# Expert networks of a two-layer decoder trunk: gathered expert rows replaced by a dense pass over the expert tables

## The chip, the cores and the metric

The kernel runs as one program on one core of a Trainium2 chip. The core has five engines that run side by side and meet through semaphores: TensorE (PE) multiplies 128-row matrices, with loaded weights on one side and up to 512 moving columns on the other, and writes to PSUM; VectorE (DVE) and ScalarE (ACT) do elementwise work; GpSimd (POOL) and SyncE (SP) issue DMA transfers here. The metric is the device time of one execution in microseconds (us); lower is better. The change touches no other core.

## The reference, cut to what matters

Two layers; each is a mixer, a cross-attention and an expert network, all in float32, for 256 tokens of width 1024. The change concerns the expert network (PEER), which for each token picks 16 experts in each of 8 heads out of 16384:

```python
q = (xi @ wq).reshape(Tb, PEER_HEADS, 2, PEER_DQ // 2)
s = jnp.einsum('thcd,hcnd->thcn', q, subkeys).astype(jnp.float32)
s1, i1 = lax.top_k(s[:, :, 0], K)          # K = 16 of 128 keys, each half
s2, i2 = lax.top_k(s[:, :, 1], K)
cand = (s1[..., :, None] + s2[..., None, :]).reshape(Tb, PEER_HEADS, K * K)
cidx = (i1[..., :, None] * PEER_NKEYS + i2[..., None, :]).reshape(Tb, PEER_HEADS, K * K)
top_s, pos = lax.top_k(cand, K)
eidx = jnp.take_along_axis(cidx, pos, axis=-1)
g = jax.nn.softmax(top_s, axis=-1)
ue = u[eidx]                               # u, v: (16384, 1024) per layer
ve = v[eidx]
act = jax.nn.gelu(jnp.einsum('td,thkd->thk', xi, ue).astype(jnp.float32), approximate=False)
return jnp.einsum('thk,thkd->td', (g * act).astype(ve.dtype), ve)
```

Each token so needs 128 rows of `u` and 128 of `v`. An expert's number is 128 * i1 + i2.

## The kernel before

Activations are kept with features on partitions (`xT`, `hT`: 8 blocks of 128 features by 256 tokens). Weights come in blocks of 2 MB through a `ring` of four, loaded by SP in the fixed order of `weight_blocks`; a block is loaded once the last PSUM job that reads the one four before it is full. All of PE's work is a list of named PSUM jobs (`psum_jobs`); job n uses bank n % 8 and waits until that bank's last user has set it free. The order of that list is PE's order.

The expert network of a layer (`peer(l)` on PE, ACT and DVE, and the GpSimd block) has two parts. First four groups g of queries: two jobs `pq` (16 float32 matmuls each, 256 columns), in the first two groups two `xr` jobs that transpose `hT` to token rows (`xrow`), and two `ps` jobs (4 matmuls each of 128 columns: the key scores of 128 tokens). DVE picks the best keys (`best_keys`), forms and sorts the candidate pairs (`candidates`, `best_pairs`, `ranks`) and turns them into expert numbers (`chosen`), two heads at a time for the first 128 tokens, and between units for the other 128.

Then 256 units per layer. A unit is one expert slot of 128 tokens, one token per partition: GpSimd gathers for each partition the 8 KB row that holds `u` and `v` of its expert (`indirect_dma_start`, 1 MB, eight slots in `arena`); DVE multiplies the `u` half by the token's row and sums it (`unit`, L1416); ACT takes Gelu, multiplies by the gate and scales an identity matrix by the result (`diag`, four buffers, L882); PE multiplies this diagonal with the `v` half, two matmuls of 512 columns, which add up over 128 units in two banks (`acc`, L516). ACT copies the sum out, PE transposes it (`back`) and DVE adds it to `xT` (L1423). The helper `mm` on PE is line L516 and the helper `fn` on ACT line L882 for every job, so that rows are told apart by their tiles. In a row of PE the names are all tiles read, in no fixed order, and one float32 `mm` stands as two records of MATMUL: the 512 units make 1024 calls of `mm` and about 2048 records.

Of the kernel before, what the change touches and what calls it, by code (L numbers as in the profile page):

```python
# [15 lines left out]
D = 1024  # L16
# [18 lines left out]
EXPERTS = PE_KEYS * PE_KEYS  # L35
# [23 lines left out]
for _name, _n in (("ident", P), ("ones", P), ("head_ones", P), ("rot", P), ("tri", P),  # L59
                  ("past", 3 * P), ("causal", 3 * P), ("iota", PE_K), ("inv_freq", 1),  # L60
                  ("levels", 8 * P)):
    CONSTS[_name] = (sum(n for _, n in CONSTS.values()), _n)
# [3 lines left out]
SLOTS = 8  # L66
UNITS = PAIRS * TT
DIAGS = 4

# [4 lines left out]
LATE_EXP = 64  # L74
BACK_LAG = 4


def constants():
# [26 lines left out]
    put("iota", np.broadcast_to(np.arange(PE_K), (P, PE_K)))  # L105
# [42 lines left out]
X_ROWS = ((0, 1), (2, 3), (), ())  # L148
# [4 lines left out]
def psum_jobs():  # L153
# [59 lines left out]
def trunk(nc, d, out_d):  # L213
# [8 lines left out]
    with ExitStack() as ctx:  # L222
# [12 lines left out]
        ring = sb("ring", [P, RING, BLOCK])  # L235
        arena = sb("arena", [P, 16384])
        vecs = sb("vecs", [P, NVEC])
        cst = sb("cst", [P, NCONST])
        w_gg = sb("w_gg", [P, KC, GLA_RANK])
        gate_up = sb("gate_up", [GLA_RANK, 2 * P])  # L240
        w_rg = sb("w_rg", [P, 2, 4, P])
# [5 lines left out]
        red = sb("red", [P, T])  # L247
        rstd = sb("rstd", [P, T])
        small = sb("small", [P, 256])
        idxT = sb("idxT", [P, T], U32)  # L250
        gateT = sb("gateT", [P, T])
        xrow = sb("xrow", [P, TT, D])
        gelus = sb("gelus", [P, SLOTS])
        gains = sb("gains", [P, SLOTS])
# [47 lines left out]

        mhV = carve(0, KC, M)
# [24 lines left out]
        late = mixT[:].rearrange("p c t -> p (c t)")  # L328
# [4 lines left out]
        s16 = sqb[:, 1024:1280].rearrange("p (c k) -> p c k", k=PE_K)  # L333
# [6 lines left out]
        i16 = rstd[:].bitcast(U32).rearrange("p (c k) -> p c k", k=PE_K)  # L340
        eidx = red[:, 0:PAIRS]

        slot = [arena[:, j * 2 * D:(j + 1) * 2 * D] for j in range(SLOTS)]

        yrow = kv[:, 0:D]
        dots = red[:, PAIRS:2 * PAIRS]

        diag = const('levels').rearrange('p (n m) -> p n m', m=P)[:, 0:DIAGS, :]

# [8 lines left out]
        in_mem = sem("in_mem")  # L358
        act_chain, dve_chain = sem("act_chain"), sem("dve_chain")
# [38 lines left out]
        routed = sem("routed")  # L398
        idx_ready = sem("idx_ready")

        gathered = [sem(f"gathered{j}") for j in range(SLOTS)]
        dotted = sem("dotted")
        gelu_done = sem("gelu_done")
        gain_done = sem("gain_done")
        weighed = sem("weighed")
        expert_mm = sem("expert_mm")
# [23 lines left out]
        def back_jobs(l):  # L430
            return [f"back{l}.{t}.{b}" for t in range(TT) for b in range(2)]

# [15 lines left out]
        def slot_of(u):  # L448
            return (u + 1) % SLOTS

        def landed(eng, l, u):

            eng.wait_ge(gathered[slot_of(u)], 16 * (l * UNITS // SLOTS + u // SLOTS + 1))

        def taken(eng, l, u):

            eng.wait_ge(expert_mm, l * UNITS + u + 1)
# [3 lines left out]
        def _(sp):  # L461
# [1319 lines left out]
```

## Time and profile before

| | us |
|---|---|
| median of 3 runs | 1932.83 |
| lowest and highest | 1928.16 and 1933.31 |
| span of the profiled execution | 1928.8 |
| PE busy | 1591.4 (83%) |
| DVE busy | 1011.3 (52%) |
| ACT busy | 646.9 (34%) |
| POOL busy | 514.9 (27%) |
| mean DMA rate | 316 GB/s |

The record has no time for the profiled execution other than its span, which lies among the times of the runs. Busy time counts records of compute instructions; matmuls overlap each other by their latency, so that busy PE means only that there was something in it. An average over the span mixes the projections, where PE works without DMA, with the two expert stages.

### The profile page before, as it was taken

Reading aid. Unit: us, or ns where it says so; the run is one execution under the profiler, and the core shown is the slowest. Engines: PE = TensorE matmul, PEld = TensorE weight load, DVE = VectorE, ACT = ScalarE, POOL = GpSimd, SP = SyncE. Lnnn points to the kernel's source line nnn. Section 1 sums busy time; section 2 is a strip of 40 time slices with the busy share of each in tenths; the row PEclk is TensorE's granted clock in tenths of the full one; section 3 lists DMA queues with packets and bytes.
Section 4 is the critical chain, followed back from the end, with each engine's and each line's share of the span. In section 5 each row is a group of like instructions: output and inputs, shape, how many; then the busy total and the mean of one; then the engine's idle time right before and its main releaser. Section 6 shows DMA issues by size and latency. Waiting matters only on the chain.

```text
span 1928.8 us, 15560 instructions
## 1 busy us (share of the span) xinstructions
PE 1591.4 (83%) x4638; PEld 806.3 (42%) x4638; DVE 1011.3 (52%) x2487; ACT 646.9 (34%) x1897; POOL 514.9 (27%) x516
## 2 busy tenths in 40 slices
PE   7999989767877877787779989997788777877876
PEld 4777778222322222222237666763232222222222
DVE  3432238688544554445441632489874445444454
ACT  1243221423433333333332433123343333333333
POOL 0000001434433433333300000015444343333331
PEclk9999999999999999999989999999999999999999
DMA  8321224999999999999933222359999999999996
GB/s 304 131 88 44 101 108 184 390 416 421 422 421 422 421 422 422 421 421 422 421 154 131 88 104 93 118 221 422 421 421 421 422 421 421 422 421 422 421 421 287
DMA packets 107540, 610.20 MB, mean 316 GB/s; under 512 B 10032, under 2 KB 10176, under 8 KB 41280
## 3 DMA queue, kind: packets, MB, share of 16 engines
q0 software_dynamic: 73728, 536.90, 67.1%
q1 hardware_dynamic: 33728, 72.30, 10.3%
q8 instruction: 37, 0.61, 0.1%
q14 instruction: 47, 0.39, 0.1%
HBM read 608.12 MB, written 1.05 MB: 316 GB/s over the span
## 4 chain that ended last, share of the span: by engine, by line
DMA 45%; PE 38%; DVE 9%; ACT 5%; issue 2%; POOL 0%; SPq 0%; DVEq 0%; PEldq 0%; ACTq 0%
DMA arena<-in_experts,idxT 45%; PE psum L516 37%; DVE arena L1416 5%; ACT cst L882 1%; ACT gains L882 1%; ACT arena L882 1%; ACT gelus L882 1%; ACT L882 1%; DVE red L1385 1%; DVE kv L1377 0%; POOL arena L1710 0%; DMA vecs<-in_vecs 0%; ACT sqb L882 0%; DVE kv L1383 0%; DVE red L1200 0%
## 5 line engine op out<-in xcount | busy, mean ns | idle before, releaser
L516 PE MATMUL psum<-arena,cst 128*128 128x512 f32 (+2 forms) x2112 | 1029.4, 616 | 283.6 <-ACT cst L882 279.1
L1416 DVE CUSTOM_DVE_ANT_0 arena<-arena,xrow 128x1024 f32<-128x1024 f32 x512 | 624.4, 1224 | 537.7 <-DMA arena<-in_experts,idxT 537.0
L1710 POOL DMA_INDIRECT arena<-in_experts,idxT x512 | 514.7, 1005 | 1387.8 <-PE psum L516 790.0
L516 PEld LDWEIGHTS psum<-arena,cst 128*128 128x128 f32 x2112 | 367.1, 191 | 942.5 <-ACT cst L882 645.7
L882 ACT ACTIVATE gelus<-red 128x1 f32<-128x1 f32 x512 | 103.6, 202 | 770.2 <-DVE red L1416 769.9
L516 PE MATMUL psum<-hT,ring 128*128 128x256 f32 x1280 | 293.3, 390 | 6.1 <-DVE hT L1215 6.1
L516 PEld LDWEIGHTS psum<-hT,ring 128*128 128x128 f32 x1280 | 248.9, 196 | 47.5 <-issue 9.8
L882 ACT ACTIVATE cst<-cst,gains 128x128 f32<-128x128 f32 x512 | 206.2, 403 | 23.2 <-PE psum L516 6.7
L882 ACT ACTIVATE gains<-gelus,gateT 128x1 f32<-128x1 f32 x512 | 150.8, 294 | 17.0 <-ACT gelus L882 0.2
L882 ACT ACTIVATE arena<-psum 128x512 f32<-128x512 f32 (+3 forms) x89 | 47.8, 545 | 304.3 <-PE psum L516 304.0
L516 PE MATMUL psum<-mixT,ring 128*128 128x256 f32 x256 | 57.4, 387 | 2.5 <-DVE mixT L1689 2.5
L516 PE MATMUL psum<-arena 64*128 64x128 f32 (+4 forms) x320 | 52.0, 317 | 4.9 <-DVE arena L1521 2.4
L516 PEld LDWEIGHTS psum<-mixT,ring 128*128 128x128 f32 x256 | 49.7, 195 | 10.8 <-DVE mixT L1689 3.3
L1223 DVE TENSOR_TENSOR xT<-xT,psum 128x512 f32<-128x512 f32 x16 | 11.0, 688 | 72.8 <-PE psum L516 72.8
L516 PE MATMUL psum<-ring,arena 128*128 128x128 f32 (+1 forms) x192 | 44.6, 384 | 2.9 <-issue 2.9
L516 PEld LDWEIGHTS psum<-arena 64*128 64x128 f32 (+2 forms) x320 | 35.7, 177 | 20.0 <-issue 10.5
L1416 DVE DVE_READ_ACCUMULATOR2_ANT red<- 128x1 f32 x512 | 42.5, 83 | 0.0
L516 PE MATMUL psum<-ring,hT 128*128 128x512 f32 x96 | 42.3, 595 | 0.0
L882 ACT ACTIVATE sqb<-xT 128x512 f32<-128x512 f32 x24 | 14.4, 625 | 81.2 <-DVE xT L1223 77.3
L516 PEld LDWEIGHTS psum<-ring,arena 128*128 128x128 f32 x192 | 27.1, 191 | 18.3 <-issue 17.8
L1533 DVE COPY_PREDICATED arena<-cst,psum 128x512 f32<-128x512 int32 x16 | 11.7, 730 | 40.7 <-PE psum L516 40.4
L516 PE MATMUL psum<-arena,ring 128*128 128x256 f32 x128 | 28.1, 380 | 1.6 <-ACT arena L882 1.6
(161 smaller groups left out, 672.1 us busy)
## 6 DMA issues: line engine op xcount, KB each, us to landing
ring<-in_peer_wq SPq DMA_DIRECT2D x8, 2048.0 KB, 8.1
ring<-in_ev_w_in SPq DMA_DIRECT2D x6, 2048.0 KB, 11.8
ring<-in_od_w_in SPq DMA_DIRECT2D x5, 2048.0 KB, 33.0
ring<-in_xa_wkv SPq DMA_DIRECT2D x4, 2048.0 KB, 7.9
arena<-in_experts,idxT POOLq DMA_INDIRECT x512, 15.3
ring<-in_ev_w_out SPq DMA_DIRECT2D x2, 2048.0 KB, 7.8
ring<-in_xa_wq SPq DMA_DIRECT2D x2, 2048.0 KB, 9.2
ring<-in_xa_wo SPq DMA_DIRECT2D x2, 2048.0 KB, 7.7
```

The costliest lines, as they stand in the source:

```text
L516: return nc.tensor.matmul(out, lhsT, rhs, start=start, stop=stop)
L882: return nc.scalar.activation(out, in_, f, **k)
L1223: V.tensor_tensor(x2, x2, pairs(o), ALU.add).then_inc(bank_free(name), 1)
L1385: link(V.tensor_reduce(eidx[:, cols], h_.rearrange("p (n c) j -> p n (c j)", c=2), X, ALU.add))
L1416: V.tensor_tensor_reduce(out=ut, in0=ut, in1=xrow[:, u // PAIRS, :], scale=1.0, scalar=0.0, op0=ALU.mult, op1=ALU.add, accum_out=dots[:, k ...
L1533: ins = V.copy_predicated(attn[:, par].rearrange("p a t q -> p (a t) q"), msk, o.rearrange("p (n q) -> p n q", q=P))
L1710: nc.gpsimd.indirect_dma_start(slot[slot_of(u)], None, d["experts"], bass.IndirectOffsetOnAxis(ap=idxT[:, u:u + 1], axis=0))\
```

## The change

The 8 KB gathers, the unit's dot products, the diagonals and the GpSimd block go. In their place all 16384 experts are computed for all 256 tokens:

- **Tables.** `keys_u` and `values_v` (64 MB each per layer) come as 128 chunks of 512 KB each, row i1 of experts per chunk, through four slots (two in `mixT`, two in `stream_tail`), issued by SP.
- **Score jobs** `pu` (64 per layer): two chunks each; for a chunk 8 matmuls, the chunk's 128x128 blocks as weights and `hT` as 256 moving columns. ACT takes Gelu of the bank into `rows_`, a field of 128 rows i1 by 256 tokens that covers `ring` and `arena`.
- **Routing.** The choice of experts keeps its instructions but gives i1, i2 and the softmax weight per slot (`picked`); three transposes per half (`tr`, after score jobs 15 and 21) turn it. From score job 22 on, `pg` jobs (64 per layer, 4 tokens each, 8 in 5 score jobs) multiply two one-hot matrices that DVE makes (`onehots`, 8 instructions of 128x128 for a job), which gives the gates of a token as a 128x128 matrix. Where the field's row is already scored DVE multiplies (`gate_rows`); for the later rows ACT copies the gates into the field, and the later scores are multiplied in (`gate_acts`).
- **Values.** After the last score job 4 matmuls with the identity put `xT` into four banks, and 128 chunks of `values_v` follow, 8 matmuls of 256 columns each, that add to the four banks (`acc`).
- **Around it.** Ring blocks are loaded in 4 parts; layer 1's first four blocks are loaded in parts between the value chunks, each part when the field's rows in its place have been read. The residual is now a copy (`whole`). The output leaves in four parts. The level masks live in `arena`, and `w_rg` is loaded after layer 0.

```diff
+STREAM = 4
+PARTS = 4
+SCORE_JOBS = PE_KEYS // 2
+GATE_TOKENS = 4
+GATE_JOBS = T // GATE_TOKENS
+EXP_AT = (9, 16)
+FLIP_AT = (15, 21)
+GATE_FROM = 22
+def gates_upto(s):
+    return min(GATE_JOBS, max(0, (8 * (s - GATE_FROM + 1) + 4) // 5))
+def gates_after(s):
+    return range(gates_upto(s - 1), gates_upto(s))
+def gated(s):
+    return GATE_TOKENS * gates_upto(s - 1)
...
     def peer(l):
         for g in range(4):
-            jobs.extend([f"pq{l}.{2 * g}", f"pq{l}.{2 * g + 1}"] + [f"xr{l}.{n}" for n in X_ROWS[g]])
-            jobs.extend([f"ps{l}.{g}", f"ps{l}.{4 + g}"])
-        jobs.extend(f"acc{l}.{t}.{b}" for t in range(TT) for b in range(2))
-        jobs.extend(f"back{l}.{t}.{b}" for t in range(TT) for b in range(2))
+            jobs.extend([f"pq{l}.{2 * g}", f"pq{l}.{2 * g + 1}", f"ps{l}.{g}", f"ps{l}.{4 + g}"])
+        for s in range(SCORE_JOBS):
+            jobs.append(f"pu{l}.{s}")
+            jobs.extend(f"tr{l}.{t}" for t in range(TT) if s == FLIP_AT[t])
+            jobs.extend(f"pg{l}.{g}" for g in gates_after(s))
+        jobs.extend(f"acc{l}.{i}" for i in range(4))
...
+            def stream(l, n):
+
+                m = n - STREAM
+                if m < 0:
+                    full(sp, "ev_out3" if l == 0 else "od_out3")
+                    if l:
+                        full(sp, f"acc{l - 1}.3")
+                elif m < PE_KEYS and m % 2:
+                    full(sp, f"pu{l}.{m // 2}")
+                elif m < PE_KEYS:
+                    sp.wait_ge(keys_read, SCORE_JOBS * l + m // 2 + 1)
                 else:
+                    sp.wait_ge(values_read, (PE_KEYS - 1) * l + m - PE_KEYS + 1)
+                table = d["keys_u"] if n < PE_KEYS else d["values_v"]
+                sp.dma_start(slots[slot_of(l, n)], table[PE_KEYS * l + n % PE_KEYS])\
+                    .then_inc(stream_in[slot_of(l, n)], 16)
...
+                for s in range(SCORE_JOBS):
+                    o, done = job(f"pu{l}.{s}")
+                    for j in range(2):
+                        u = streamed(pe, l, 2 * s + j).rearrange("p (k e) -> p k e", e=P)
+                        for k in range(KC):
+                            last = mm(o[:, j * T:(j + 1) * T], u[:, k, :], hT[:, k, :], k == 0, k == KC - 1)
+                        last.then_inc(done if j else keys_read, 1)
...
+                    for g in gates_after(s):
+                        pe.wait_ge(hot_ready, GATE_JOBS * l + g + 1)
+                        o, done = job(f"pg{l}.{g}")
+                        for j in range(GATE_TOKENS):
+                            last = mm(o[:, j * P:(j + 1) * P], onehot[:, g % 2, 0, j, :], onehot[:, g % 2, 1, j, :])
                         last.then_inc(done, 1)
-                for t in range(TT):
-                    (o0, done0), (o1, done1) = job(f"acc{l}.{t}.0"), job(f"acc{l}.{t}.1")
-                    for k in range(PAIRS):
-                        u = t * PAIRS + k
-                        pe.wait_ge(weighed, l * UNITS + u + 1)
-                        v = slot[slot_of(u)][:, D:2 * D]
-                        first = mm(o0, diag[:, u % DIAGS, :], v[:, 0:BANK], k == 0, k == PAIRS - 1)
-                        last = mm(o1, diag[:, u % DIAGS, :], v[:, BANK:D], k == 0, k == PAIRS - 1)
...
+                acc = [job(f"acc{l}.{i}") for i in range(4)]
+                for i in range(4):
+                    mm(acc[i][0], ident, xT[:, 2 * i:2 * i + 2, :].rearrange("p c t -> p (c t)"), True, False)
+                copied(pe, f"pg{l}.{GATE_JOBS - 1}", f"pu{l}.{GATED_FROM - 1}")
+                for i in range(PE_KEYS):
+                    if i // 2 >= GATED_FROM:
+                        pe.wait_ge(acts_gated, GATED_JOBS * l + i // 2 - GATED_FROM + 1)
+                    v = streamed(pe, l, PE_KEYS + i)
+                    for c in range(KC):
+                        o, done = acc[c // 2]
+                        last = mm(o[:, c % 2 * T:(c % 2 + 1) * T], v[:, c * P:(c + 1) * P], rows_[:, i, :],
+                                  False, i == PE_KEYS - 1 and c % 2 == 1)
...
+                def onehots(g):
+
+                    if g >= 2:
+                        n = JOB[f"pg{l}.{g - 2}"]
+                        dve.wait_ge(psum_full[n % BANKS], n // BANKS + 1)
+                    copied(dve, f"tr{l}.{GATE_TOKENS * g // P}")
+                    for j in range(GATE_TOKENS):
+                        t = GATE_TOKENS * g + j
+                        step(V.tensor_scalar(onehot[:, g % 2, 0, j, :], const("iota"), pickT[:, 1, t:t + 1], None, ALU.is_equal))
+                        ins = V.tensor_scalar(onehot[:, g % 2, 1, j, :], const("iota"), pickT[:, 0, t:t + 1],
+                                              pickT[:, 2, t:t + 1], ALU.is_equal, ALU.mult)
...
+                def gate_rows(s, g):
+
+                    o = full(dve, f"pg{l}.{g}").rearrange("p (t i) -> p i t", i=PE_KEYS)
+                    dve.wait_ge(gate_copied, GATE_JOBS * l + g + 1)
+                    copied(dve, f"pu{l}.{s}")
+                    x_ = rows_[:, 0:2 * s + 2, GATE_TOKENS * g:GATE_TOKENS * (g + 1)]
+                    V.tensor_tensor(x_, x_, o[:, 0:2 * s + 2, :], ALU.mult).then_inc(bank_free(f"pg{l}.{g}"), 1)
...
+                for s in range(GATE_FROM, SCORE_JOBS):
+                    if gated(s):
+                        gate_acts(s)
+                    for g in gates_after(s):
+                        gate_rows(s, g)
+                        if g + 2 < GATE_JOBS:
+                            onehots(g + 2)
```

On PE, at the end of layer 0's queries and in its expert stage, the kernel before has these rows (`psum<-` names the tiles read; `hT,ring` is a `pq` job, `ring,arena` a `ps` job, `arena,cst` the units, `cst,kv` a `back` job; one row counts calls of `mm`):

```order
L516 MATMUL psum<-hT,ring 128x256 x32
L516 MATMUL psum<-ring,arena 128x128 x8
L516 MATMUL psum<-hT,ring 128x256 x32
L516 MATMUL psum<-ring,arena 128x128 x8
L516 MATMUL psum<-arena,cst 128x512 x268
L663 MATMUL psum<-cst,kv 128x128 x8
L516 MATMUL psum<-arena,cst 128x512 x244
L663 MATMUL psum<-cst,kv 128x128 x8
```

The changed kernel has there, at the end of the score jobs and the start of the values (`hT,mixT` and `hT,stream_tail` are `pu` jobs, `sqb` the one-hot products of `pg`, `xT,cst` the identity matmuls, `field` the rows of activations):

```order
L577 MATMUL psum<-hT,mixT 128x256 x16
L577 MATMUL psum<-sqb 128x128 x8
L577 MATMUL psum<-hT,stream_tail 128x256 x16
L577 MATMUL psum<-sqb 128x128 x4
L577 MATMUL psum<-hT,mixT 128x256 x16
L577 MATMUL psum<-hT,stream_tail 128x256 x16
L577 MATMUL psum<-xT,cst 128x512 x4
L577 MATMUL psum<-field,mixT 128x256 x16
L577 MATMUL psum<-field,stream_tail 128x256 x16
```

Where 512 calls of 512 columns stood per layer, there stand 64 groups of 16 calls of 256 columns for the scores, 64 groups of 4 calls of 128 columns for the gates, 4 of 512 columns, and 128 groups of 8 calls of 256 columns for the values.

On DVE, in the same stretch of score jobs, the changed kernel has rows of this kind (`field<-field,kv` is `gate_acts`, `field<-field,psum` is `gate_rows`, `sqb<-cst,pick` are the one-hots, eight of them before the next `gate_rows`):

```order
L1480 TENSOR_TENSOR field<-field,kv 128x2x104
L1472 TENSOR_TENSOR field<-field,psum 128x78x4
L1459 TENSOR_SCALAR sqb<-cst,pick 128x128
L1460 TENSOR_SCALAR sqb<-cst,pick 128x128
L1459 TENSOR_SCALAR sqb<-cst,pick 128x128
```

They take the place of the dot products (L1416) of the units, 256 a layer.

## Rows read from the trace of the kernel before

**Rows 1.** The page, parts 1 and 2: busy time; DMA rate in 40 slices

```profile
PE 1591.4 (83%) x4638; PEld 806.3 (42%) x4638; DVE 1011.3 (52%) x2487; ACT 646.9 (34%) x1897; POOL 514.9 (27%) x516
GB/s 304 131 88 44 101 108 184 390 416 421 422 421 422 421 422 422 421 421 422 421 154 131 88 104 93 118 221 422 421 421 421 422 421 421 422 421 422 421 421 287
```

**Rows 2.** The page, part 4: the chain that ended last, by engine

```profile
DMA 45%; PE 38%; DVE 9%; ACT 5%; issue 2%; POOL 0%; SPq 0%; DVEq 0%; PEldq 0%; ACTq 0%
```

**Rows 3.** Groups of instructions by line and shape, whole span

```profile
L516 PE MATMUL psum<-arena,cst 128*128 128x512 f32 x2064 | 1018.2, 622 | 283.6 <-ACT cst L882 279.1 <-ACT arena L882 4.4
L1416 DVE CUSTOM_DVE_ANT_0 arena<-arena,xrow 128x1024 f32<-128x1024 f32 x512 | 624.4, 1224 | 537.7 <-DMA arena<-in_experts,idxT 537.0
L516 PE MATMUL psum<-hT,ring 128*128 128x256 f32 x1280 | 293.3, 390 | 6.1 <-DVE hT L1215 6.1
```

**Rows 4.** The timeline of expert units, steady state of layer 0

```profile
599.33 1.98 PE L516 MATMUL psum<-arena,cst 128*128 128x512 f32 x4 [0.51 <-ACT cst L882]
599.53 1.23 DVE L1416 CUSTOM_DVE_ANT_0 arena<-arena,xrow 128x1024 f32<-128x1024 f32 x1 [1.25 <-DMA arena<-in_experts,idxT]
601.81 1.98 PE L516 MATMUL psum<-arena,cst 128*128 128x512 f32 x4 [0.50 <-ACT cst L882]
```

**Rows 5.** Busy time in the two expert stages (columns named in the row)

```profile
core 0: us, PE busy (x) PEld busy (x) DVE busy (x) ACT busy (x) POOL busy (x), PEclk, DMA share, GB/s
338.30:1001.70 663.40, 511.28 (x1043) 180.62 (x1042) 375.72 (x829) 244.47 (x791) 248.53 (x249) 0.98 0.98 407
1283.90:1928.80 644.90, 504.14 (x1041) 179.74 (x1040) 371.97 (x820) 239.34 (x781) 252.93 (x249) 0.99 0.98 407
```

**Rows 6.** The timeline of PE, end of layer 0's queries

```profile
302.24 1.04 PE L644 MATMUL psum<-cst,hT 128*128 128x128 f32 x8
303.14 2.02 PE L516 MATMUL psum<-ring,arena 128*128 128x128 f32 x16
305.00 13.98 PE L516 MATMUL psum<-hT,ring 128*128 128x256 f32 x64
319.71 2.02 PE L516 MATMUL psum<-ring,arena 128*128 128x128 f32 x16 [0.73 <-issue]
```

**Rows 7.** The timeline of PE in layer 1's mixer

```profile
1037.95 3.60 PE L516 MATMUL psum<-sqb,cst 128*128 128x512 f32 x8
1041.39 7.07 PE L516 MATMUL psum<-hT,ring 128*128 128x256 f32 x32
```

**Rows 8.** Busy time and granted clock, two stretches (columns as in rows 5)

```profile
270.00:275.00 5.00, 5.00 (x14) 4.00 (x13) 1.69 (x5) 0.00 (x0) 0.00 (x0) 0.54 0.32 116
1045.00:1085.00 40.00, 40.00 (x151) 27.21 (x150) 18.49 (x39) 8.73 (x15) 0.00 (x0) 1.00 0.40 142
```

**Rows 9.** Groups of instructions by line and shape, VectorE, whole span

```profile
L1223 DVE TENSOR_TENSOR xT<-xT,psum 128x512 f32<-128x512 f32 x16 | 11.0, 688 | 72.8 <-PE psum L516 72.8
L1650 DVE TENSOR_SCALAR sqb<-sqb,small 128x128 f32<-128x128 f32 x8 | 2.3, 286 | 0.3
```

**Rows 10.** The timeline of VectorE: first and last instruction routing two heads

```profile
287.73 0.89 DVE L1293 MAX8 sqb<-psum 128x8 f32<-128x128 f32 x4 [16.04 <-PE psum L516]
...
301.59 0.18 DVE L1386 CAST idxT<-red 128x32 uint32<-128x32 f32 x1
```

**Rows 11.** The page, part 6: DMA issues, size and time to landing

```profile
arena<-in_experts,idxT POOLq DMA_INDIRECT x512, 15.3
ring<-in_subkeys SPq DMA_DIRECT2D x2, 1024.0 KB, 4.9
```

**Rows 12.** The timeline between a projection's end and the next, layer 0

```profile
264.31 0.69 DVE L1223 TENSOR_TENSOR xT<-xT,psum 128x512 f32<-128x512 f32 x1 [1.97 <-PE psum L516]
269.07 1.19 PE L516 MATMUL psum<-hT,ring 128*128 128x256 f32 x2 [1.53 <-DVE hT L1215]
```

**Rows 13.** The timeline of the kernel's last expert work and output

```profile
1919.63 1.98 PE L516 MATMUL psum<-arena,cst 128*128 128x512 f32 x4 [0.47 <-ACT cst L882]
1924.48 0.36 SPq L492 DMA_DIRECT2D out<-xT  x1
```

More of the change, by code:

```diff
@@ L34 @@
 PE_H, PE_K, PE_KEYS, PE_DQ = 8, 16, 128, 128
-EXPERTS = PE_KEYS * PE_KEYS
 PAIRS = PE_H * PE_K
@@ L339, in trunk @@
         row_a, row_at, line = sqb[:, 1792:1920], sqb[:, 1920:2048], sqb[:, 1536:1664]
[L340 to L348, printed above, removed]
+        onehot = sqb[:].rearrange("p (b c j n) -> p b c j n", b=2, c=2, j=GATE_TOKENS)
+        acts = kv[:].rearrange("p (b i t) -> p b i t", i=2, t=T)
+        slots = [mixT[:, 0:4, :].rearrange("p c t -> p (c t)"), mixT[:, 4:8, :].rearrange("p c t -> p (c t)")]
+        slots += [stream_tail[:, j, :] for j in range(STREAM - 2)]
         psum = ctx.enter_context(nc.psum_tensor("psum", [P, BANKS, BANK], F))
@@ L397, in trunk @@
         top_exp = sem("top_exp")
[L398 to L406, printed above, removed]
+        picked_ready = sem("picked_ready")
+        stream_in = [sem(f"stream_in{j}") for j in range(STREAM)]
+        keys_read, values_read = sem("keys_read"), sem("values_read")
+        hot_ready = sem("hot_ready")
+        gate_copied = sem("gate_copied")
+        acts_gated = sem("acts_gated")
         stored = sem("stored")
@@ L486, in _ @@
             load(3)
-            sp.dma_start(w_rg[:], d["rg_gates"]).then_inc(in_mem, 16)
             sp.dma_start(sinT[:].bitcast(I32), d["positions"].to_broadcast([P, T])).then_inc(in_mem, 16)
-            for b in range(RING, len(BLOCKS)):
+            first = AT["od_mq"]
+            for b in range(RING, AT["pq02"]):
                 load(b)
-            copied(sp, "back1.1.0", "back1.1.1")
-            sp.dma_start(out_d, xT[:]).then_inc(stored, 16)
-            sp.wait_ge(stored, 16)
+            for n in range(STREAM):
+                stream(0, n)
+            for b in range(AT["pq02"], first):
+                load(b)
+            for n in range(STREAM, 2 * PE_KEYS):
+                stream(0, n)
+                i, ahead = divmod(n - PE_KEYS - 40, 4)
+                if ahead == 0 and 0 <= i < RING * PARTS:
+                    b = first + i // PARTS
+                    if i % PARTS == 0:
+                        sp.wait_ge(values_read, BLOCK // T * (b % RING + 1))
+                    part(b, i % PARTS)
+            full(sp, "acc0.3")
+            sp.dma_start(w_rg, d["rg_gates"]).then_inc(in_rg, 16)
+            for b in range(first + RING, AT["pq12"]):
+                load(b)
+            for n in range(STREAM):
+                stream(1, n)
+            for b in range(AT["pq12"], len(BLOCKS)):
+                load(b)
+            for n in range(STREAM, 2 * PE_KEYS):
+                stream(1, n)
+            for i in range(4):
+                copied(sp, f"acc1.{i}")
+                sp.dma_start(out_d[:, 2 * i:2 * i + 2, :], xT[:, 2 * i:2 * i + 2, :]).then_inc(stored, 16)
+            sp.wait_ge(stored, 64)
         @block.tensor
@@ L1010, in peer, with exponentials, activate @@
-                rows_out(1)
+                def exponentials(t):
+                    act.wait_ge(top_ready, TT * l + t + 1)
+                    fn(top, top, ACT.Exp).then_inc(top_exp, 1)
+                def activate(s):
+                    n = gated(s)
+                    o = full(act, f"pu{l}.{s}").rearrange("p (i t) -> p i t", t=T)
+                    if n < T:
+                        ins = fn(rows_[:, 2 * s:2 * s + 2, n:], o[:, :, n:], ACT.Gelu)
+                    if n:
+                        m = s - GATED_FROM
+                        if m >= 4:
+                            act.wait_ge(acts_gated, GATED_JOBS * l + m - 3)
+                        ins = fn(acts[:, m % 4, :, 0:n], o[:, :, 0:n], ACT.Gelu)
+                    ins.then_inc(bank_free(f"pu{l}.{s}"), 1)
@@ new lines, in peer @@
+                for s in range(SCORE_JOBS):
+                    activate(s)
+                    for t in range(TT):
+                        if s == EXP_AT[t]:
+                            exponentials(t)
+                        if s == FLIP_AT[t]:
+                            copy_out(f"tr{l}.{t}", pickT[:, :, t * P:(t + 1) * P])
+                    for g in gates_after(s):
+                        o = full(act, f"pg{l}.{g}").rearrange("p (t i) -> p i t", i=PE_KEYS)
+                        ts = slice(GATE_TOKENS * g, GATE_TOKENS * (g + 1))
+                        fn(rows_[:, 2 * s + 2:, ts], o[:, 2 * s + 2:, :], ACT.Copy).then_inc(gate_copied, 1)
@@ L1593, in _ @@
             peer(0)
+            residual(parts("acc0.", 4), "od", whole=True)
             norm("od", xT, vec("od_norm"), hT, h_ready)
```

331 lines of the change are left out of this document (121 added, 210 removed).

## The prediction

> **What bounds the kernel now.** I read the page first: PE is busy 83% of the span, DVE half of it, and the DMA rate stands at 421 GB/s in two long plateaus [rows 1]. The chain that ended last gives 45% of the span to one transfer, the gather of expert rows, and 38% to PE [rows 2]. The groups say what each engine waited for: the dot products for the gather (537.0 us), the diagonal matmuls for ACT (279.1 us), which itself stands behind the dot product [rows 3]. The timeline settles it: units start 2.48 us apart (599.33 to 601.81), and in that time PE has 1.98 us of records and DVE 1.23 us; DVE waits 1.25 us for the DMA each time [rows 4]. 1 MB in 2.48 us is 422 GB/s, the plateau. So the two expert stages, 663.4 us in layer 0 (end of the last key scores to the first matmul of the next projection) and 644.9 us in layer 1 (to the end), are bound by DMA [rows 5]; 256 x 2.48 = 635 us of each is gathers. The other 620.5 us of the span are projections and attention, which the change hardly touches.
>
> The bytes halve: 128 MB for a layer instead of 256 MB. At 422 GB/s that is 318 us. The question is whether PE can follow, so what matters is the price of one float32 matmul.
>
> **The price of a matmul.** Where nothing interrupts PE, the end of the queries, 64 records of 128x256 last 13.98 us in all [rows 6]; one record has 0.390 us from issue to end [rows 3], so starts are (13.98 - 0.39) / 63 = 215.7 ns apart. The 32 records in rows 7 give (7.07 - 0.39) / 31 = 215.5. The code issues 640 calls of `mm` with `hT` and a ring block at 256 columns, and the trace has 1280 records [rows 3]: one call is two records, 431.4 ns. The units count the same way, 1024 calls and some 2048 records. For 512 columns, 8 records take 3.44 us to the next row's start [rows 7], 0.86 us a call. For 128 columns, 16 records from 303.14 to 305.00 are 0.2325 us a call [rows 6]. The transposes are one record each, 8 in 0.90 us [rows 6].
>
> The Trainium skill, "FP8 and Floating Point Precision", TensorE Precision Notes, says that true FP32 takes four passes through the array, and "TensorE: Matmul & The Clock Gate", section "Wait — 56ns, not 53.3ns?", puts a warm matmul of N columns at N / 2.4 GHz plus about 2.5 ns. By four such passes a call of 256 columns would be an estimated 4 x 109.2 = 437 ns, which makes the sum below 22 us longer; by a single pass it would be 109 ns and the change would win widely. The measured 431.4 sides with four passes, and the sum goes by it.
>
> **What is added, per layer.** All new `mm` calls of the scores have the form of the queries (128x128 weights from SBUF, `hT` as 256 moving columns), and the values have the same shape with the field's row as moving side:
> - scores 64 x 16 and values 128 x 8 = 2048 calls x 0.4314 = 883.5 us
> - gates 64 x 4 = 256 calls x 0.2325 = 59.5 us
> - 6 transposes 0.7 us, 4 identity calls x 0.86 = 3.4 us
> - together 947.1 us of PE, without a gap.
>
> **What hides the rest.** Transfers: a chunk of 512 KB is used up in 8 x 0.4314 = 3.45 us, 152 GB/s. A slot is refilled while PE is on the other three, 10.35 us. The nearest direct load, 1 MB, lands in 4.9 us [rows 11], so this is hidden, also with the weight parts between them. DVE in the gate stretch: for five score jobs there are eight `pg` jobs. Per score job 12.8 one-hots of 128x128 at most 0.286 us each = 3.66 us, 1.6 `gate_rows` and one `gate_acts` of at most 0.69 us each = 1.79 us [rows 9]: 5.5 us, while PE takes 16 x 0.4314 + 6.4 x 0.2325 = 8.4 us. The order also fits: after a `pg` is full, its `gate_rows` and the one-hots of the job after the next follow in about 3 to 6 us, and a score job of 6.9 us lies between. Routing: two heads of 128 tokens take DVE 14.0 us [rows 10], eight such parts 112 us; they start with the first key scores, some 50 us before the score jobs, so that both halves could be ready 62 us into them. The exponentials hold them back (ACT does them after score jobs 9 and 16, at 69 and 117 us), but PE asks for the halves only after jobs 15 and 21, at 110 and 152 us. ACT has two Gelu halves and at most two copies in 8.4 us. I cost all of this at nothing. The four `xr` transposes per layer, 0.90 us for two of them, save little, since the key scores behind them have to wait 0.73 us for ACT where they are absent [rows 6]: 0.17 x 4 = 0.7 us in all.
>
> **The seams.** After layer 0's values comes the chain copy, squares, sums, norm, normalise. The same chain after a projection took from 264.31 to 269.07, 4.8 us [rows 12]. Layer 0: 947.1 + 4.8 = 951.9 instead of 663.4, +288.5 us. In layer 1 the last matmul is followed by one copy (0.69 us) and 256 KB of output. The 1 MB output was issued at 1924.48 and the span ended at 1928.8 [rows 13], 4.3 us; for less data I take 3.3, so a tail of 4 us. Layer 1: 951.1 instead of 644.9, +306.2 us.
>
> Sum: 1928.8 + 288.5 + 306.2 - 0.7 = 2522.8 us against the profiled span. The median of the runs shown is 4 us above that span; I take half of it: **2525 us**, 31% slower. The gathers were moving bytes that the dense form partly saves, but it trades 635 us of DMA for 947 us of PE.
>
> **The rivals.**
> - *The mean of the group instead of the uninterrupted pace.* All 1280 records occupy 293.3 us [rows 3], 0.458 a call, with the clock's dips and gated starts in it. Against it: the dips stand behind idle time (granted clock 0.54 at 270 to 275 us, after the wait of rows 12), and 40 us without a gap show 1.00 [rows 8]. The new stage has no idle stretch. If 256 stops for a chunk's semaphore per layer cost something, it would come out here: 4096 x 0.027 = +110, 2633 us. 60 ns a chunk would give +31, 2556. Chance 12% for something over 2585.
> - *The chunks come late.* If a chunk took the 15.3 us of the gathers [rows 11], a round of four would take 18.75 us instead of 13.8, 1.24 us more a chunk, 512 chunks: +634, 3160 us. It decides from 10.35 us on. The 15.3 belongs to up to eight transfers of 1 MB in flight at 421 GB/s; here at most four of half the size at 152. 2%.
> - *DVE or ACT bounds the gate stretch.* The field is written in runs of four elements, 1 KB apart, and PSUM is read across; no row has such a form. If `gate_rows` cost five times its row, DVE would need 9.9 us for PE's 8.4: +1.5 x 40 x 2 = +120, 2645 us. It decides from 2.5 us an instruction on, 3.6 times the row. 4%.
> - *The clock.* With PE granted its lower level, 1.2 GHz (0.50), over the whole stage every call doubles: some 4400 us. Nothing in the rows shows that without idle time ahead. 1%.
> - *Not slower.* If one `mm` of the new form were one record, not two, PE would need 2048 x 0.2157 + 63.6 = 505 us a layer, still above the 318 us of DMA, and the time would be 1928.8 - 1308.3 + 2 x 505 + 8.8 - 0.7 = 1639 us. It decides where a call costs less than (1308.3 + 0.7 - 8.8 - 127.2) / 4096 = 0.286 us. For it speaks only that the moving side of the values is new; against it every float32 group of the trace, the diagonals included, which have two records a call. 1%.
>
> **The numbers.** The sum as worked out holds with 80%: its own bounds are 2505 (tail and seam shorter, the 0.43 us a call to the third digit, the 0.2325 of the gates 10% high, the start a little shorter by the split loads) and 2585 (60 ns a chunk, a few dips after seams, 10 us of stalls while the gate stretch starts). The rest lies above, but for 1% below. Range 2500 to 2590. A measurement of this kernel tells 0.3% (6 us) from no change; by these cases faster has 1%, within it 1%, slower 98%.
>
> **What would show it.** In the profile after: the expert stages 950 us each; PE busy near 100% there with the clock at 1.00; 64 records in about 13.8 us also for `hT,mixT`; DMA at 150 GB/s in them; no wait of PE on the streams, on `hot_ready` or `picked_ready` worth more than a few us; DVE about 65% busy between the first `pg` and the last; the chain that ended last nearly all PE. Wrong would make it: records with another pace than 216 ns, waits of PE on a DMA of `mixT` or `stream_tail`, or on DVE's one-hots; or 1280-record counting that doesn't hold, so that the new stages have half the records.

## The result, and the profile after

The changed kernel took 2522.99 us (median of 4 runs, 2521.83 to 2524.73) against 1930.79 us for the kernel before beside it (4 runs, 1928.16 to 1933.31). The ratio is 1.3068, with an interval of 1.3048 to 1.3088: slower by 31%. The profiled span is 2522.9 us; 2525 was predicted, with a range of 2500 to 2590.

The page of the changed kernel, busy time, DMA rate in 40 slices and the chain that ended last, answers to [rows 1, 2]:

```profile
PE 2467.5 (98%) x11770; PEld 2119.1 (84%) x11770; DVE 685.1 (27%) x2503; ACT 297.4 (12%) x669; POOL 0.2 (0%) x4
GB/s 258 110 58 139 78 89 154 143 133 124 127 126 126 142 150 177 198 184 184 153 90 116 99 118 34 151 150 138 130 126 126 125 126 151 155 154 150 152 155 135
PE 97%; DVE 1%; ACT 1%; issue 1%; DMA 0%; SPq 0%; DVEq 0%
```

The plateau of 421 GB/s is gone. Nothing but PE is left in the chain, and DMA, which had 45% of it, has 0%. The groups by line and shape show the new work and how often each record stands (answers to [rows 3]; two more groups of 2048, with the other names, have the same means):

```profile
L577 PE MATMUL psum<-hT,mixT 128*128 128x256 f32 x2048 | 452.6, 379 | 0.0
L577 PE MATMUL psum<-field,stream_tail 128*128 128x256 f32 x2048 | 452.5, 379 | 0.0
L577 PE MATMUL psum<-sqb 128*128 128x128 f32 x1024 | 127.2, 275 | 0.0
L1460 DVE TENSOR_SCALAR sqb<-cst,pick 128x128 f32<-128x128 f32 x512 | 173.7, 339 | 0.0
L1459 DVE TENSOR_SCALAR sqb<-cst,pick 128x128 f32<-128x128 f32 x512 | 142.6, 278 | 0.1
```

4096 calls of 256 columns gave 8192 records: two for a call, as counted before. The last column, the idle time ahead of the group, is the strongest line of the page: in 8192 records on streamed chunks PE never waited. The price of a call stands in the timeline of PE in the changed kernel, in the gate stretch and in the values:

```profile
497.60 1.95 PE L577 MATMUL psum<-sqb 128*128 128x128 f32 x16
499.39 7.07 PE L577 MATMUL psum<-hT,stream_tail 128*128 128x256 f32 x32
506.30 1.95 PE L577 MATMUL psum<-sqb 128*128 128x128 f32 x16
508.08 7.07 PE L577 MATMUL psum<-hT,mixT 128*128 128x256 f32 x32
```

A score job of 16 calls takes 499.39 to 506.30, 6.91 us, 0.432 a call. Two gate jobs (8 calls) take 506.30 to 508.08, 1.78 us, 0.2225 a call. By the same reading a call of 512 columns takes 0.86 us (837.95 to 841.38 below, four calls). All three have 128x128 weights, so the price goes with the columns that move and not with the weights that are loaded. The windows of the changed kernel, over the scores, over the gate stretch, and over the values (columns as in rows 5):

```profile
338.00:830.00 492.00, 492.00 (x2533) 439.97 (x2532) 218.04 (x855) 66.10 (x173) 0.00 (x0) 1.00 0.42 134
516.00:800.00 284.00, 284.00 (x1530) 255.91 (x1529) 137.36 (x522) 39.84 (x123) 0.00 (x0) 1.00 0.40 127
840.00:1280.00 440.00, 440.00 (x2037) 386.69 (x2036) 0.00 (x0) 0.66 (x4) 0.00 (x0) 1.00 0.52 168
```

PE is busy for the whole of every window at a granted clock of 1.00, the 2.4 GHz level. DVE is busy 137.36 of 284 us in the gate stretch, 48%. The DMA issues of the page, size and time to landing, answer to [rows 11]:

```profile
mixT<-in_keys_u SPq DMA_DIRECT2D x128, 512.0 KB, 3.4
stream_tail<-in_values_v SPq DMA_DIRECT2D x128, 512.0 KB, 3.5
```

The borders of the stages stand in the timeline: first scores, identity calls, values, the seam, the first scores of layer 1, and the end (kernel after, answers to [rows 6, 12, 13]):

```profile
338.09 7.07 PE L577 MATMUL psum<-hT,mixT 128*128 128x256 f32 x32
...
837.95 3.60 PE L577 MATMUL psum<-xT,cst 128*128 128x512 f32 x8
841.38 7.07 PE L577 MATMUL psum<-field,mixT 128*128 128x256 f32 x32
...
1276.50 7.07 PE L577 MATMUL psum<-field,stream_tail 128*128 128x256 f32 x32
1286.73 0.70 PE L577 MATMUL psum<-sums,cst 128*128 128x256 f32 x2 [3.16 <-DVE sums L1259]
...
1573.98 7.07 PE L577 MATMUL psum<-hT,mixT 128*128 128x256 f32 x32
...
2519.51 0.69 DVE L1740 COPY xT<-psum 128x512 f32<-128x512 f32 x1 [0.17 <-PE psum L577]
```

The stage of layer 0 goes from 338.09 to the next projection's first matmul at 1288.96, 950.9 us; from there to layer 1's scores it is 285.0 us; layer 1's stage is 1573.98 to 2522.9, 948.9 us.

### The profile page after: what moved, and what is told of

Read it like the earlier page. It is cut to its first block, busy times and chain, and to the rows that moved or that the text cites. A ratio compares the mean times of both kernels' runs of the same rounds, so it can differ in the third digit from the quotient of the medians.

```text
span 2522.9 us, 28446 instructions
## 1 busy us (share of the span) xinstructions
PE 2467.5 (98%) x11770; PEld 2119.1 (84%) x11770; DVE 685.1 (27%) x2503; ACT 297.4 (12%) x669; POOL 0.2 (0%) x4
## 4 chain that ended last, share of the span: by engine, by line
PE 97%; DVE 1%; ACT 1%; issue 1%; DMA 0%; SPq 0%; DVEq 0%
PE psum L577 96%; ACT field L949 1%; DMA vecs<-in_vecs 0%; ACT sqb L949 0%; DVE sums L1259 0%; DVE sums L1258 0%; ACT sums L949 0%; DVE small L1314 0%; DVE field L1680 0%; ACT L949 0%; DVE field L1728 0%; PE psum L665 0%; DVE hT L1274 0%; DVE small L1683 0%; DVE small L1682 0%
## 5 line engine op out<-in xcount | busy, mean ns | idle before, releaser
L577 PE MATMUL psum<-hT,mixT 128*128 128x256 f32 x2048 | 452.6, 379 | 0.0
L577 PE MATMUL psum<-hT,stream_tail 128*128 128x256 f32 x2048 | 452.6, 379 | 0.0
L577 PE MATMUL psum<-field,stream_tail 128*128 128x256 f32 x2048 | 452.5, 379 | 0.0
L577 PE MATMUL psum<-field,mixT 128*128 128x256 f32 x2048 | 452.5, 379 | 0.0
L577 PEld LDWEIGHTS psum<-field,mixT 128*128 128x128 f32 x2048 | 389.1, 190 | 53.8 <-issue 1.0
L577 PEld LDWEIGHTS psum<-field,stream_tail 128*128 128x128 f32 x2048 | 389.1, 190 | 52.9
L577 PEld LDWEIGHTS psum<-hT,stream_tail 128*128 128x128 f32 x2048 | 386.1, 190 | 50.8
L577 PEld LDWEIGHTS psum<-hT,mixT 128*128 128x128 f32 x2048 | 385.6, 190 | 50.5
L577 PE MATMUL psum<-hT,field 128*128 128x256 f32 x1280 | 295.8, 393 | 6.1 <-DVE hT L1274 6.1
L1460 DVE TENSOR_SCALAR sqb<-cst,pick 128x128 f32<-128x128 f32 x512 | 173.7, 339 | 0.0
L1459 DVE TENSOR_SCALAR sqb<-cst,pick 128x128 f32<-128x128 f32 x512 | 142.6, 278 | 0.1
L1480 DVE TENSOR_TENSOR field<-field,kv 128x512 f32<-128x512 f32 (+39 forms) x82 | 36.2, 441 | 344.8 <-ACT kv L949 344.8
```

The costliest lines, as they stand in the source:

```text
L577: return nc.tensor.matmul(out, lhsT, rhs, start=start, stop=stop)
L1459: step(V.tensor_scalar(onehot[:, g % 2, 0, j, :], const("iota"), pickT[:, 1, t:t + 1], None, ALU.is_equal))
L1460: ins = V.tensor_scalar(onehot[:, g % 2, 1, j, :], const("iota"), pickT[:, 0, t:t + 1], pickT[:, 2, t:t + 1], ALU.is_equal, ALU.mult)
L1480: V.tensor_tensor(x_, x_, acts[:, m % 4, :, 0:n], ALU.mult).then_inc(acts_gated, 1)
```

## The experiments

The theory: a float32 call of 256 columns costs PE 0.431 us of its own, and 4096 of them are the whole loss; the transfers, DVE and ACT lie beside it with room. The rivals: the loss, or part of it, is in how the chunks arrive or in what DVE must make. A second question is why the old kernel stood where it did. Each run was timed beside the kernel before on the same chip. The edits are shown by their main lines; "..." stands for lines left out.

### The values in bf16

GpSimd loads pairs of chunks with a cast to bf16 (1 MB read, 512 KB written), the field is bf16, and the values' 1024 calls a layer run on bf16 operands; scores and gates stay float32 up to the field. The result is rounded accordingly. The narrower field leaves the ring free, so layer 1's first four weight blocks are loaded whole, from the eighth pair of layer 0's values on.

```diff
-        rows_ = field[:].rearrange("p (i t) -> p i t", t=T)
+        rows_ = arena.bitcast(BF).rearrange("p (i t) -> p i t", t=T)
...
+                    nc.gpsimd.dma_start(pair_slots[at % STREAM], table[i:i + 2].rearrange("i p d -> p i d"))\
+                        .then_inc(pair_in[at % STREAM], 16)
...
```

> Only the value matmuls are given bfloat16 operands: the field of activations is written as bfloat16, and GpSimd issues the value chunks in pairs (1 MB read, cast on the way). The scores stay float32. Theory (a float32 call is two records and 431 ns because of its type, and PE alone sets the expert stage): a bfloat16 call is one record of well under 216 ns, so that the transfer takes over as the bound of the value part: 64 pairs x 2.48 us = 159 us for a layer in place of 442, 2523 - 2 x 283 = 1957 us; value part with PE waiting for DMA. Rival A (the pace belongs to loading 128x128 weights, about 190 ns a load): 64 x 16 x 0.19 = 195 us, 2029 us, PE without a gap. Rival B (a cast transfer issued by GpSimd runs at half the rate): 317 us for a layer, 2273 us. Rival C (pace independent of the type): 2523 us.

Measured: 1982.84 us (1981.88 to 1983.8, 2 runs), ratio 1.0271 (1.025 to 1.0291). That is 540 us less than the changed kernel, from one half of its calls. The timeline of PE in this kernel, layer 1, from the last score job into the values:

```profile
1807.90 7.07 PE L601 MATMUL psum<-hT,stream_tail 128*128 128x256 f32 x32
1814.80 3.60 PE L601 MATMUL psum<-xT,cst 128*128 128x512 f32 x8
1818.24 3.66 PE L601 MATMUL psum<-field,mixT 128*128 128x256 bf16 x32
1821.73 3.66 PE L601 MATMUL psum<-field,stream_tail 128*128 128x256 bf16 x32
1826.04 1.92 PE L601 MATMUL psum<-field,mixT 128*128 128x256 bf16 x16 [0.66 <-DMA mixT<-in_values_v]
```

And in layer 0, while the weight blocks come in beside the values:

```profile
885.70 1.92 PE L601 MATMUL psum<-field,stream_tail 128*128 128x256 bf16 x16 [1.97 <-DMA stream_tail<-in_values_v]
889.59 1.92 PE L601 MATMUL psum<-field,mixT 128*128 128x256 bf16 x16 [1.97 <-DMA mixT<-in_values_v]
```

In the first list the first and the fourth row have the same shape and the same number of records, 7.07 us against 3.66: records now start 109 ns apart ((1821.73 - 1818.24) / 32), and a call has one record instead of two. After four pairs PE is ahead of the transfers and waits, so that the rivals fall: under rival A PE would have no gap, and B and C are 290 us and more above the measured time. The total is 26 us above what was expected, and most of it can be read in the trace: layer 0's values took from 841.27 to 1023.71, 182.4 us, layer 1's from 1818.24 to about 1977.4, 159 us. The 64 MB of a table at 422 GB/s are 159 us. Beside layer 0's values come the next layer's first four weight blocks, 8 MB or 20 us at that rate. They are issued from 858.53 on, and from there to about 925 the pairs start some 3.9 us apart instead of 2.48 (second list). In the changed kernel they are read under a PE that is busy anyway. I had left them out of a stage that this edit made DMA-bound. A speedup of PE turned hidden bytes into time.

### Scores in bf16 too

The edit before stays, and the scores run on bf16 keys, cast on the way, and a bf16 copy of `hT`.

```diff
+        at_b = [ring[:, AT[f"sub{l}"] % RING, 2048:3072].bitcast(BF).rearrange("p (k t) -> p k t", t=T) for l in range(LAYERS)]
...
-                            last = mm(o[:, j * T:(j + 1) * T], u[:, k, :], hT[:, k, :], k == 0, k == KC - 1)
+                            last = mm(o[:, j * T:(j + 1) * T], u[:, k, :], at_b[l][:, k, :], k == 0, k == KC - 1)
```

> Scores and values both have bfloat16 operands (a bfloat16 copy of the normalised activations for the scores; keys and values cast on the way, GpSimd issues them in pairs). Routing, gates and all else stay float32. Theory: PE no longer bounds the score part; DVE does, with 112 us of routing of which 50 lie before the score jobs, 512 one-hots at 0.23 us and 64 products, some 60 + 118 + 40 = 220 us, and values at the transfer's pace 159 us: 385 us for a layer in place of 947, total about 1400 us, faster than the kernel before by a quarter or more. Rival (one of the float32 parts that are left keeps PE as the bound, or the cast transfers run at half rate): 640 us for a layer, 1900 us or more.

Measured: 1412.4 us (1410.67 to 1415.61, 4 runs), ratio 0.7313 (0.7301 to 0.7325). The same dense plan, with the same number of calls and the same table bytes read, is 27% below the old kernel once the calls on the tables cost 109 ns. The old kernel keeps float32 operands in this comparison; no run has gathers with bf16 operands. What bounds it now differs by stretch. The timeline of PE in this kernel, in the values, and what PE waited for (us in total, times, longest):

```profile
648.60 1.91 PE L606 MATMUL psum<-field,mixT 128*128 128x256 bf16 x16 [0.56 <-DMA mixT<-in_values_v]
651.08 1.91 PE L606 MATMUL psum<-field,mixT 128*128 128x256 bf16 x16 [0.57 <-DMA mixT<-in_values_v]
```

```profile
PE psum L606 <- DMA mixT<-in_values_v: 47.6, 60, 2.1
PE psum L606 <- DMA stream_tail<-in_values_v: 45.0, 60, 2.0
PE psum L606 <- DVE sqb L1492: 36.1, 46, 1.3
```

Pairs are 2.48 us apart, the same 1 MB in 2.48 us that the gathers had [rows 4]. In the values PE waits for DMA; in the gate stretch it waits for DVE's one-hots, which the float32 calls had covered.

### A quarter of the gate products

```diff
                     for g in gates_after(s):
...
-                        for j in range(GATE_TOKENS):
+                        for j in range(1):
```

This leaves out PE's gate products of three tokens in four.

> Each gate job on PE multiplies the one-hots of one of its four tokens; the gates of the other three are left out (what stands in the bank is used). All waits and all work of DVE and ACT stay. Theory (PE bounds the gate stretch): 3/4 of the gates' 256 calls go, 2 x 192 x 0.2225 = 85 us less, 2438 us. Rival (DVE or the handshake of PE, ACT and DVE sets the pace of the stretch and PE's one-hot products are covered): 2523 us, or at most 20 us less.

Measured: 2436.53 us (2436.42 to 2436.64, 2 runs), ratio 1.2621 (1.2595 to 1.2646). It is 86.5 us less, for 384 calls of 128 columns less: 0.225 us a call. The whole of what is left out comes back, so PE sets the time in this stretch also, and it is the product's own price.

### DVE's one-hots three times

```diff
-                    for j in range(GATE_TOKENS):
+                    for n, j in enumerate([0, 1, 2, 3] * 3):
+                        if n in (GATE_TOKENS, 2 * GATE_TOKENS):
+                            settle()
...
```

Each one-hot is made three times over, with the same values. `settle` is a wait of DVE for its own last instruction, twice in each job.

> DVE makes every one-hot three times, with the same result. Theory (DVE is covered by PE, about 4.1 us of 8.35 us a score job in the gate stretch): DVE then needs 3 x 2.9 + 1.2 = 9.9 us a score job and a little more for its waits, and becomes the bound by 1.5 to 2.5 us, 40 score jobs in each layer: +120 to +200 us, 2640 to 2720 us, with PE waiting for DVE only in this stretch. Rival (DVE was at its limit already): + 2 x 40 x 5.8 = 464 us or more, 2990 us.

Measured: 2662.4 us (2661.83 to 2662.96, 2 runs), ratio 1.3791 (1.3763 to 1.3818). PE's wait for the one-hots in this kernel, and a window of its gate stretch (columns as in rows 5):

```profile
PE psum L577 <- DVE sqb L1462: 91.2, 43, 3.9
```

```profile
800.00:860.00 60.00, 53.72 (x252) 47.30 (x253) 59.37 (x236) 5.33 (x19) 0.00 (x0) 0.89 0.28 88
```

DVE is now busy for 59.37 us of the 60. Only what goes beyond PE's time is paid: in the changed kernel DVE has some 4.1 us in a score job's 8.4 (48%), of which 6.4 pairs of one-hots are 2.9 (a pair starts every 0.45 us, below); with three times the pairs DVE has 9.8 us. 1.4 us over in each of some 80 score jobs gives about 112 us, and 139 were measured. Most of the rest is the edit's own: around each `settle` the next one-hot starts 0.13 us later than within a round (699.97 to 700.35 is 0.38 us, where 524.88 to 525.13 in the changed kernel is 0.25), twice in each of 128 jobs, 33 us. PE's waits are only 91.2 us; its score and gate records take some 50 us longer in all, at a granted clock of 0.89 to 0.97 in the windows of this stretch, where the changed kernel has 1.00. By the same numbers the cover over DVE ends at about 2.5 times the present one-hots ((8.4 - 1.2) / 2.9), an estimate that no run tests; the changed kernel did not use it up.

### Two slots instead of four

```diff
-STREAM = 4
+STREAM = 2
...
-        stream_tail = sb("stream_tail", [P, STREAM - 2, D])
```

> The float32 dense kernel with two stream slots in place of four; the rest as it is. A slot is then refilled while PE is on one other chunk, 3.45 us (with four: 10.35 us). Theory (a chunk lands in about 3.5 us, so four slots cover it three times over): a turn of two chunks takes max(6.9, 3.45 + 3.5 + some 0.3 for the semaphores and the issue) = 7.2 us, +0.1 to 0.3 us a chunk, 512 chunks: 2555 to 2680 us, with short waits of PE for the streams. Rival (a chunk in flight alone is as slow as the gathers were, 15.3 us): a turn of 18.8 us, some 3000 us more.

Measured: 2638.2 us (2636.89 to 2639.51, 2 runs), ratio 1.3662 (1.3634 to 1.3689): 115 us more, 0.225 us for each of 512 chunks. The waits of PE in this kernel, and two rows of its timeline in layer 0's values:

```profile
PE psum L576 <- DMA mixT<-in_values_v: 36.2, 78, 1.4
PE psum L576 <- DMA mixT<-in_keys_u: 17.5, 39, 1.3
```

```profile
860.58 7.07 PE L576 MATMUL psum<-field,mixT 128*128 128x256 f32 x32
867.81 7.17 PE L576 MATMUL psum<-field,mixT 128*128 128x256 f32 x32 [0.16 <-DMA mixT<-in_values_v]
```

The waits come to 53.7 us and not to 115, because a record counts until its end: the two rows start 7.23 us apart instead of 6.91, 0.32 us lost, and 0.16 stands as wait. A chunk lands in 3.5 us and the other slot lasts PE 3.45 us, so two slots fall short by a little each time, and four, with a window of 10.35 us, have three times what they need. So the rival of the late chunks was out by a margin.

### The old kernel with half a dot product

The dot product of each unit reads 512 of 1024 elements; half of it is left out.

```diff
-                    V.tensor_tensor_reduce(out=ut, in0=ut, in1=xrow[:, u // PAIRS, :], scale=1.0, scalar=0.0,
+                    ut = ut[:, 0:D // 2]
+                    V.tensor_tensor_reduce(out=ut, in0=ut, in1=xrow[:, u // PAIRS, 0:D // 2], scale=1.0, scalar=0.0,
```

> The gather kernel of before, with the dot product of each unit over the first 512 of 1024 columns only (the other half is left out); gathers unchanged. Theory (its expert stage is bound by the bytes, 1 MB in 2.48 us): 1930 us as before, DVE waits longer. Rival (it is bound by the turn of its eight slots: 15.3 us to land and some 4.5 us through DVE, ACT and PE): the turn is 0.5 us shorter, 0.06 us a unit, 1900 us.

Measured: 1929.99 us (1928.49 to 1931.68, 10 runs), ratio 0.9995 (0.9985 to 1.0004). The timeline of DVE in two units of this kernel, against [rows 4], and its DMA issues, against [rows 11]:

```profile
597.72 0.69 DVE L1417 CUSTOM_DVE_ANT_0 arena<-arena,xrow 128x512 f32<-128x512 f32 x1 [1.78 <-DMA arena<-in_experts,idxT]
...
600.22 0.69 DVE L1417 CUSTOM_DVE_ANT_0 arena<-arena,xrow 128x512 f32<-128x512 f32 x1 [1.79 <-DMA arena<-in_experts,idxT]
```

```profile
arena<-in_experts,idxT POOLq DMA_INDIRECT x512, 15.9
```

The 0.54 us that DVE gained went into its wait (1.25 to 1.78), and the units stay some 2.5 us apart. A slot came free earlier, but no gather landed sooner: from issue to landing it now takes 15.9 us instead of 15.3. The rival of the slots' turn (1900 us) is out, and the transfers themselves are the bound of the old stages, as read.

### One-hots and iota in bf16, on top of all-bf16 tables

```diff
-                        step(V.tensor_scalar(onehot[:, g % 2, 0, j, :], const("iota"), pickT[:, 1, t:t + 1], None, ALU.is_equal))
...
+                        step(V.tensor_scalar(onehot[:, g % 2, 0, j, :], iota_wide[:], pickT[:, 1, t:t + 1], None, ALU.is_equal))
...
```

Here the gates too are rounded to bf16.

> As e2 (scores and values in bfloat16), and the one-hots, with the softmax weight in one of them, are bfloat16 too. In e2 the gate stretch is DVE's: 174 us for 40 score jobs, 4.35 us each, PE waiting for the one-hots. Theory (the one-hots' time on DVE is what counts; with two-byte elements it falls from 0.23 us to 0.10 to 0.18 each, the gate product on PE from 0.93 to 0.25 us a job): 2.7 to 3.5 us a score job, 35 to 65 us less a layer, 1280 to 1340 us; below 2.5 us a score job the transfer takes over. Rival (an instruction of 128 elements costs its fixed part, whatever the type; only PE's part shrinks): 1400 us or at most 15 us less.

Measured: 1375.19 us (1372.72 to 1376.89, 4 runs), ratio 0.7124 (0.7112 to 0.7136). It is the fastest version found, 37 us below the one before it, and it lies between what the theory and its rival gave. I had expected DVE's one-hots to get much cheaper in bf16. The timeline of DVE, first in the changed kernel (float32), then in this one:

```profile
524.68 0.28 DVE L1459 TENSOR_SCALAR sqb<-cst,pick 128x128 f32<-128x128 f32 x1
524.88 0.34 DVE L1460 TENSOR_SCALAR sqb<-cst,pick 128x128 f32<-128x128 f32 x1
525.13 0.28 DVE L1459 TENSOR_SCALAR sqb<-cst,pick 128x128 f32<-128x128 f32 x1
```

```profile
440.79 0.25 DVE L1492 TENSOR_SCALAR sqb<-iota_bf,pick 128x128 bf16<-128x128 bf16 x1
440.96 0.31 DVE L1493 TENSOR_SCALAR sqb<-iota_bf,pick 128x128 bf16<-128x128 bf16 x1
441.18 0.25 DVE L1492 TENSOR_SCALAR sqb<-iota_bf,pick 128x128 bf16<-128x128 bf16 x1
```

A pair of one-hots starts every 0.45 us in float32 and every 0.39 us in bf16. Of 0.225 us an instruction, 0.195 did not change with the type; what it consists of no run here tells apart. The waits of PE in this kernel, and the window of its gate stretch (columns as in rows 5):

```profile
PE psum L607 <- DVE sqb L1493: 76.0, 56, 2.0
```

```profile
400.00:530.00 130.00, 92.29 (x877) 74.75 (x875) 129.83 (x599) 41.61 (x142) 28.00 (x40) 0.97 0.92 157
```

DVE is busy 129.83 of 130 us there and PE waits for it more than before (76.0 against 36.1 us), since its own gate products got cheaper.

## Why the prediction was right, point by point

**The bound of before and the bytes.** DMA-bound at 422 GB/s: shown by the halved dot product, which left the time as it was, and by the bf16 versions, in which 1 MB again takes 2.48 us.

**The price of a float32 call.** Predicted 0.4314 us from the uninterrupted pace of [rows 6, 7], measured 6.91 / 16 = 0.4319 in the scores and 442.0 / 1024 = 0.4316 in the values (841.38 to 1283.4). This term is 93% of the new stages, and it carried the result. The rival of the group mean (0.458) came out wrong, but dips of the clock were only part of the reason. In the new kernel, with a granted clock of 1.00 and no stop, the same mean still gives 0.442 us a call (452.6 / 1024), because every row counts its last record to the end (7.07 us against 6.91 to the next row's start). A chunk's semaphore costs nothing that shows. The bf16 row confirms the mechanism: the same call costs 109 ns, 3.95 times less, and the loss turns into a gain of 27%.

The Trainium skill, "FP8 and Floating Point Precision", TensorE Precision Notes, gives true FP32 four passes; the ratio of 3.95 sits beside it. The Trainium skill, "TensorE: Matmul & The Clock Gate", section "Wait — 56ns, not 53.3ns?", works out to an estimated 109.2 ns for 256 columns, and the bf16 call's 109 agrees; for float32 the trace decides for 431.4 ns rather than the estimate of 437, so that the extra 2.5 ns do not seem to come four times.

**The gates.** Predicted 59.5 us a layer, measured 57.0 (256 x 0.2225). The row that I took had a seam to other jobs in its 1.86 us. Scores, gates and transposes: 502.0 predicted, 499.9 measured (338.09 to 837.95). Identity 3.4 and 3.4.

**What hides the rest.** It was hidden, with more room than I gave it. A chunk of 512 KB lands in 3.4 to 3.5 us; I had taken the 4.9 of a load of 1 MB. DVE has about 4.1 us of work in a score job's 8.4, not 5.5 (48%, not 65%): I priced a one-hot at 0.286 us, its time from issue to end, but such instructions overlap and start 0.225 us apart, 0.8 us less for the 12.8 of them. It is the same slip that I avoided on PE. The remaining 0.6 us lie in the products, which I had priced at 0.69 us each by a larger row. It cost nothing here, since PE was above it either way, and it would have misplaced the point where DVE decides, which lies at about 2.5 times the present one-hots. PE waited before none of the 12 transposes that take up the routing's result.

**The seams.** Layer 0's took 5.4 us (1283.57 to 1288.96), 4.8 predicted; the tail 3.4, 4 predicted. Layer 0's stage: 950.9 against 951.9. Layer 1's: 948.9 against 951.1.

**What was not predicted.** The part between the layers was to become 0.35 us shorter (half of the 0.7), and the profile has it 2.8 us longer: 282.2 us before (1001.73 to 1283.92), 285.0 after. The windows just behind the seam show where, first in the changed kernel, then before:

```profile
1289.00:1294.00 5.00, 5.00 (x12) 3.98 (x13) 3.17 (x11) 0.00 (x0) 0.00 (x0) 0.50 0.00 0
1294.00:1299.00 5.00, 5.00 (x22) 4.25 (x22) 0.00 (x0) 0.00 (x0) 0.00 (x0) 0.89 0.00 0
```

```profile
1002.00:1007.00 5.00, 5.00 (x17) 4.14 (x17) 2.95 (x10) 0.00 (x0) 0.00 (x0) 0.70 0.00 0
1007.00:1012.00 5.00, 5.00 (x25) 4.41 (x24) 0.00 (x0) 1.23 (x2) 0.00 (x0) 1.00 0.01 3
```

The same matmuls got a clock of 0.50 and 0.89 where before they got 0.70 and 1.00, and the projection took 37.6 us to 1326.60 instead of 36.2 to 1037.95: 1.4 us. A second dip gives the rest: 16 records at 1381.34 take 4.94 us, and the same 16 at 1092.28 before took 3.72.

Nothing ties this to the change. The run with triple one-hots has the same values stage, the same seam (PE idle for 3.16 and 1.53 us) and the same code between the layers, and there the windows behind the seam are:

```profile
1360.00:1365.00 5.00, 4.93 (x16) 4.15 (x17) 3.27 (x11) 0.00 (x0) 0.00 (x0) 0.69 0.00 0
1365.00:1370.00 5.00, 5.00 (x25) 4.41 (x24) 0.00 (x0) 1.23 (x2) 0.00 (x0) 1.00 0.00 0
```

Its projection took 36.1 us and the whole part 281.8 us, the predicted 0.35 below the kernel before. With a quarter of the gate products the part took 283.0 us, with two slots 284.9. So one profiled execution differs from another by up to 3.2 us in this part alone, by when the clock comes back; what decides that is not settled by any run.

The sum: the two expert stages came out 1.0 and 2.2 us shorter than worked out, and the rest of the span 3.3 us longer, nearly all of it between the layers. These cancel, and 2522.9 measured stands against 2522.8 worked out. That the last digit agrees is chance; that each expert stage is within 0.3% of what was worked out is not.

## What to carry to other kernels

Price a new matmul by the pace of an uninterrupted run of the same type and shape in your own trace, starts divided by count, and ask how many records one call makes, before counting what a dense form saves in bytes: halving the bytes is worth nothing if float32 products then take 3.45 us for a chunk that DMA brings in 1.24. When the fast operand type takes PE away as the bound, look for what lay under it: here hidden weight blocks (20 us) and DVE's one-hots (36 to 76 us of waits) came up at once. Small elementwise instructions are to be priced start to start, not from issue to end, and a narrower type may save little on them (13% here); no run tried fewer of them.

## What the runs showed of the hardware that was not expected

- After the same values stage at a granted clock of 1.00 and the same seam of about 5 us, in which PE was idle for 3.16 and 1.53 us, the next two windows of 5 us had 0.50 and 0.89 in the profile of one kernel and 0.69 and 1.00 in that of another. With a second dip later, the same code took from 281.8 to 285.0 us.
- A load that casts float32 to bf16 on its way reads at the same rate as a plain one: 1 MB in 2.48 us, 422 GB/s read. The DMA rate in the window of such a stretch counts the bytes written and so shows half; the first scores with both tables in bf16, where 211 GB/s in the last column go with a DMA share of 1.12:

```profile
345.00:390.00 45.00, 34.05 (x287) 26.95 (x288) 43.73 (x190) 16.88 (x25) 12.84 (x18) 1.00 1.12 211
```

- A one-hot of 128x128 starts 0.225 us after the last in float32 and 0.195 us in bf16, a gain of 13% for half the bytes.
- A wait that the profile shows for PE is shorter than the time lost, since the last record runs on into it: 0.16 us shown for 0.32 lost, above.
